# Causal latent attention of a prompt: the value product turned round and given to halves of the TensorE array, the weight sums carried with it, and three engines' turns rearranged

## The reference

```
q = (rmsnorm(cq) @ w_qb)              # 64 + 32 columns a head; the 32 are rotated
s = q_lat . ckv + q_pe . kpe          # masked where k_pos > q_pos, times MLA_SCALE
p = softmax(s)                        # over the keys
o_lat = p @ ckv ; o = o_lat @ w_uv    # 64 columns a head
```

## Time and profile before

| | us |
|---|---|
| median of 3 runs | 3236.84 (3233.66 to 3237.91) |
| the profiled execution | 3235.72 |
| its span | 3234.1 |

### The profile page before, as it was taken

One profiled execution on the slowest core, in us unless ns is written; L12 is line 12 of the kernel. 1 busy time (PEld: TensorE's weight loads), 2 busy tenths in 40 slices (PEclk: granted clock), 3 DMA queues, 4 the chain that ended last, 5 costly groups with the idle time before them and its releaser, 6 DMA issues. The chain is left out here.

```text
span 3234.1 us, 51727 instructions
## 1 busy us (share of the span) xinstructions
PE 3056.2 (95%) x21218; PEld 2736.5 (85%) x21218; DVE 1802.0 (56%) x3078; ACT 929.1 (29%) x1550; POOL 244.0 (8%) x280
## 2 busy tenths in 40 slices
PE   6987899998999999999989779989999999999998
PEld 5975577667999999999979546776699999999998
DVE  4856677553454545544566757865535545444554
ACT  4034444552311111111220444445423111111113
POOL 2000001540000000000020000025300000000000
PEclk8986999999999999999989779999999999999998
DMA  4112101762111111111031310047521111111201
GB/s 104 46 38 55 21 5 54 253 220 68 33 53 40 46 53 52 47 40 40 23 51 38 65 39 7 5 136 232 168 62 40 52 47 53 47 40 40 59 28 71
DMA packets 226587, 207.99 MB, mean 64 GB/s; under 512 B 50260, under 2 KB 195796, under 8 KB 226148
## 3 DMA queue, kind: packets, MB, share of 16 engines
q1 hardware_dynamic: 200744, 119.38, 13.6%
q0 software_dynamic: 25600, 85.11, 8.5%
HBM read 193.58 MB, written 11.05 MB: 63 GB/s over the span
## 5 line engine op out<-in xcount | busy, mean ns | idle before, releaser
L189 PE MATMUL ps<-streamH,upH 128*128 128x344 f32 x2112 | 449.2, 321 | 6.3 <-issue 5.0
L189 PE MATMUL ps<-streamH,upL 128*128 128x344 f32 x2112 | 447.4, 320 | 0.0
L189 PE MATMUL ps<-streamL,upH 128*128 128x344 f32 x2112 | 446.1, 320 | 0.0
L2266 ACT ACTIVATE upH<-hc 128x1024 fp32r<-128x1024 f32 x88 | 93.4, 1061 | 967.7 <-PE ps L189 967.7
L189 PEld LDWEIGHTS ps<-streamH,upH 128*128 128x128 f32 x2112 | 354.6, 188 | 8.7 <-issue 6.4
L189 PEld LDWEIGHTS ps<-streamH,upL 128*128 128x128 f32 x2112 | 356.1, 189 | 0.0
L189 PEld LDWEIGHTS ps<-streamL,upH 128*128 128x128 f32 x2112 | 352.8, 188 | 0.0
L2430 DVE TENSOR_TENSOR xT<-xT,ps 128x1032 f32<-128x1032 f32 x176 | 216.0, 1228 | 227.6 <-PE ps L189 227.6
L443 PE MATMUL ps<-inH,inW 128*128 128x344 f32 (+1 forms) x1248 | 234.1, 323 | 31.3 <-DVE inW L497 31.3
L2391 DVE TENSOR_TENSOR hc<-ps,rstd 128x1032 f32<-128x1032 f32 x44 | 54.2, 1232 | 370.7 <-PE ps L189 370.7
L443 PEld LDWEIGHTS ps<-inH,inW 128*128 128x128 f32 (+1 forms) x1248 | 198.9, 183 | 38.4 <-DVE inW L497 32.3
(11 more groups left out here) (472 smaller groups left out, 4899.4 us busy)
## 6 DMA issues: line engine op xcount, KB each, us to landing
hc<-in_w_ffn_in SPq DMA_DIRECT2D x88, 512.0 KB, 4.6
hc<-in_w_ffn_out SPq DMA_DIRECT2D x44, 512.0 KB, 3.7
big<-in_w_in SPq DMA_DIRECT2D x22, 512.0 KB, 3.9
stream_raw<-in_w_out SPq DMA_DIRECT2D x16, 512.0 KB, 4.0
big<-in_x_prompt SPq DMA_DIRECT2D x2, 2048.0 KB, 9.9
out_y_prompt<-big SPq DMA_DIRECT2D x8, 512.0 KB
scratch_y<-hc SPq DMA_DIRECT2D x16, 136.0 KB, 3.2
scratch_u<-wring SPq DMA_DIRECT2D x4, 516.0 KB, 3.1
```

What stands on the lines that cost most here:

```text
L189: last = pe.matmul(self.ps[:, bank + n, 0:NCOL], w, x[:, n * NCOL:(n + 1) * NCOL], start=(k == 0 and i == 0), stop=(k == len(terms) - 1 an ...
L2266: act.activation(upH[u][:, :, :], raw[u], ACT.Copy).then_inc(g_wh[u], 1)
```

## The change

- Four units make a **group**: `order` is now, for j = 0 to 3, for each head z, the blocks q = 7-j and q = j. Within a group the units A, B, C, D are (head 0, large), (head 0, small), (head 1, large), (head 1, small).
- `values(i)` works for a whole group. The 64 columns of `vt` are stationary (128 x 64), and p^T moves (128 columns). Head 0 writes partitions 0 to 63 of bank 7 and head 1 partitions 64 to 127, so each works on half of the array's columns, their products written in turn. The result has features on partitions. `outputs` and `otok` go away.
- The reciprocal of a row's sum must then lie along the columns: `reciprocals(u)` writes it 64 times over (128 x 64 from a broadcast source) to `rden`; `values(i)` first turns the two 128 x 128 tiles of `rden` into bank 7; ACT `factors(i)` copies them to `rT` (256 columns); DVE `output(i)` multiplies bank 7 by `rT` straight into `hc` (256 columns).
- p^T of a group is kept in four tiles, filled afresh only when the values of the group before are done. DVE `copies` takes the first bank of a large unit (512 columns), ACT `copies` all others.
- Scores run three units ahead: even units in banks 0 to 3, odd ones (at most 512 columns) in bank 4; p^T goes through banks 5 and 6; bank 7 is shared by the values and the steps, each of which waits until what was there before is drained.
- Ten steps instead of eleven: keys in two pieces of 512 columns instead of three of up to 344. They stand at units 0, 1, 2, 4, 5, 6, 8, 9, 10 and 12 of a pair.

```diff
-        otok = [take(D_MODEL).rearrange("p (q c) -> p q c", q=QT) for _ in range(2)]
+        small_pT = [take(512) for _ in range(2)]
+        rden = [take(P) for _ in range(2)]
+        rT = take(2 * P)
...
-        prob, pT = [T(16), T(17)], [T(18), T(19)]
...
-        order = [(v % 2, QT - 1 - v // 2 if v % 2 == 0 else v // 2) for v in range(NV)]
+        order = [(z, q) for j in range(4) for z in range(2) for q in (QT - 1 - j, j)]
...
-        STEPS = "DAAADDDAAAD"
+        copied_by = ["DA"[g] if u % 2 == 0 else "A" for u in range(NU) for g in range(banks_of[u])]
+        STEPS = "DAAADDDAAD"
         NS = len(STEPS)
-        step_at = {v: v - 2 for v in range(2, 1 + NS)}
-        step_at[NS + 2] = NS - 1
+        step_at = {v: j for j, v in enumerate((0, 1, 2, 4, 5, 6, 8, 9, 10, 12))}
+        VALUES_BANK = 7
...
+        step_of, values_of = {(0, j): j for j in range(NS)}, []
+        for u in range(NU):
+            p, v = u // NV, u % NV
+            if v in step_at and p + 1 < PAIRS:
+                step_of[p + 1, step_at[v]] = len(kinds)
+                kinds += STEPS[step_at[v]]
+            if v % 4 == 3:
+                values_of.append(len(kinds))
+                kinds += "V"
...
+        def copied(eng, at):
+            eng.wait_ge({"A": e_ta, "D": e_te}[copied_by[at]], copied_by[:at + 1].count(copied_by[at]))
+
+        def score_banks(u):
+            return ps[:, 2 * (u // 2 % 2):2 * (u // 2 % 2) + 2, :].rearrange("p b n -> p (b n)") if u % 2 == 0 else ps[:, 4, :]
+
+        def slot(kind, u):
+            return st[:, 4 * kind + u % 4:4 * kind + u % 4 + 1]
         chunk = lambda c: slice(c * NCOL, (c + 1) * NCOL)
-        kchunk = lambda c: slice(c * NCOL, min((c + 1) * NCOL, SEQ))
+        kchunk = lambda c: slice(c * 512, (c + 1) * 512)
...
-                    elif j in (7, 8, 9):
+                    elif j in (7, 8):
...
-                def outputs(p, half):
-                    k = out_of[p, half]
-                    drained(pe, k - 1)
-                    pe.wait_ge(e_oe, NV * p + (12, 16)[half])
-                    for i, q in enumerate(((2, 3, 4, 5), (0, 1, 6, 7))[half]):
-                        last = pe.transpose(ps[:, 7, i * P:(i + 1) * P], otok[p % 2][:, q, :], ident)
-                    last.then_inc(e_ax, 1)
...
-                    if u >= 2:
+                    if u % 2 == 0 and u >= 4:
+                        pe.wait_ge(e_p, u - 3)
+                    if u % 2 == 1 and u >= 2:
                         pe.wait_ge(e_p, u - 1)
...
-                        last = pe.matmul(ps[:, 2 * (u % 2) + c // 512, 0:w], query[p % 2][z][0:KQ, q * P:(q + 1) * P],
+                        last = pe.matmul(score_banks(u)[:, c:c + w], query[p % 2][z][0:KQ, q * P:(q + 1) * P],
...
-                            pe.wait_ge(e_te, at - 1)
+                            copied(pe, at - 2)
...
-                def values(u):
-                    p, z, q = units[u]
-                    pe.wait_ge(e_te, first_bank[u + 1])
-                    if u >= 1:
-                        pe.wait_ge(e_oe, u)
-                    h = 2 * p + z
-                    for kb in range(q + 1):
-                        last = pe.matmul(ps[:, 6, 0:V_DIM], pT[u % 2][:, kb * P:(kb + 1) * P], vt[:, kb, h * V_DIM:(h + 1) * V_DIM],
-                                         start=(kb == 0), stop=(kb == q))
+                def values(i):
+                    p, j = i // 4, i % 4
+                    drained(pe, values_of[i] - 1)
+                    pe.wait_ge(e_r, 4 * i + 4)
+                    for w in range(2):
+                        pe.transpose(ps[:, VALUES_BANK, (2 * w + 1) * P:(2 * w + 2) * P], rden[w], ident)
+                    for at in (first_bank[4 * i + 4] - 1, first_bank[4 * i + 2], first_bank[4 * i + 3] - 1):
+                        copied(pe, at)
+                    for w, q in ((1, QT - 1 - j), (0, j)):
+                        for kb in range(q + 1):
+                            for z in range(2):
+                                h = 2 * p + z
+                                last = pe.matmul(ps[64 * z:64 * z + 64, VALUES_BANK, 2 * w * P:(2 * w + 1) * P], vt[:, kb, h * V_DIM:(h + 1) * V_DIM],
+                                                 pT[w][z][:, kb * P:(kb + 1) * P], start=(kb == 0), stop=(kb == q))
                     last.then_inc(e_o, 1)
...
-                scores(0)
-                scores(1)
+                for u in range(3):
+                    scores(u)
...
                 for u in range(NU):
                     p, v = u // NV, u % NV
                     transposes(u)
-                    if u + 2 < NU:
-                        scores(u + 2)
-                    if u >= 1:
-                        values(u - 1)
-                    if v == 1 and p:
-                        outputs(p - 1, 1)
+                    if u + 3 < NU:
+                        scores(u + 3)
                     if v in step_at and p + 1 < PAIRS:
                         step(p + 1, step_at[v])
-                    if v == 14:
-                        outputs(p, 0)
-                values(NU - 1)
-                outputs(PAIRS - 1, 1)
+                    if v % 4 == 3:
+                        values(u // 4)
...
-
-                def outputs(p, half):
...
+                    if u >= 4:
+                        act.wait_ge(e_r, u - 3)
...
-                def output(u):
+                    act.activation(prob[u % 2][:, 0:n], score_banks(u)[:, 0:n], ACT.Exp, bias=slot(0, u), scale=MLA_SCALE,
+                                   accum_out=slot(1, u)).then_inc(e_p, 1)
+
+                def copies(u):
                     p, z, q = units[u]
-                    act.wait_ge(e_r, u + 1)
-                    act.wait_ge(e_o, u + 1)
-                    act.activation(otok[p % 2][:, q, z * V_DIM:(z + 1) * V_DIM], ps[:, 6, 0:V_DIM], ACT.Copy,
-                                   scale=st[:, 4 + u % 2:5 + u % 2]).then_inc(e_oe, 1)
-                for j in (1, 2, 3, 7, 8, 9):
+                    if u // 4:
+                        act.wait_ge(e_o, u // 4)
+                    for g in range(banks_of[u]):
+                        at = first_bank[u] + g
+                        w = (min(4 * g + 4, q + 1) - 4 * g) * P
+                        if copied_by[at] == "A":
+                            act.wait_ge(e_t, at + 1)
+                            act.activation(pT[1 - u % 2][z][:, 4 * g * P:4 * g * P + w], ps[:, 5 + at % 2, 0:w], ACT.Copy).then_inc(e_ta, 1)
+
+                def factors(i):
+                    act.wait_ge(e_o, i + 1)
+                    if i:
+                        act.wait_ge(e_oe, i)
+                    act.activation(rT.rearrange("p (w c) -> p w c", w=2),
+                                   ps[:, VALUES_BANK, :].rearrange("p (w x c) -> p w x c", w=2, x=2)[:, :, 1, :], ACT.Copy).then_inc(e_rt, 1)
+                for j in (1, 2, 3, 7, 8):
...
                 for u in range(NU):
                     p, v = u // NV, u % NV
-                    if u >= 1:
-                        output(u - 1)
+                    if u and u % 4 == 0:
+                        factors(u // 4 - 1)
+                    copies(u)
                     if u + 2 < NU:
                         exponentials(u + 2)
-                    if v == 1 and p:
-                        outputs(p - 1, 1)
                     if v in step_at and p + 1 < PAIRS and STEPS[step_at[v]] == "A":
                         drain(p + 1, step_at[v])
-                    if v == 14:
-                        outputs(p, 0)
-                output(NU - 1)
-                outputs(PAIRS - 1, 1)
+                factors(NU // 4 - 1)
...
-                    two = ps[:, 2 * (u % 2):2 * (u % 2) + 2, :].rearrange("p b n -> p (b n)")
+                    two = score_banks(u)
...
+                    s.link(dve.reduce_max(slot(2, u), two[:, 0:n], AX))
...
                 def reciprocals(u):
+                    p, z, q = units[u]
                     dve.wait_ge(e_p, u + 1)
-                    if u >= 2:
-                        dve.wait_ge(e_oe, u - 1)
-                    dve.reciprocal(st[:, 4 + u % 2:5 + u % 2], st[:, 2 + u % 2:3 + u % 2]).then_inc(e_r, 1)
+                    if u // 4:
+                        dve.wait_ge(e_o, u // 4)
+                    dve.reciprocal(rden[1 - u % 2][:, 64 * z:64 * z + 64], slot(1, u).to_broadcast([P, 64])).then_inc(e_r, 1)

                 def copies(u):
-                    p, z, q = units[u]
-                    for g in range(banks_of[u]):
-                        at = first_bank[u] + g
-                        w = (min(4 * g + 4, q + 1) - 4 * g) * P
-                        dve.wait_ge(e_t, at + 1)
-                        if u >= 2:
-                            dve.wait_ge(e_o, u - 1)
-                        dve.tensor_copy(pT[u % 2][:, 4 * g * P:4 * g * P + w], ps[:, 4 + at % 2, 0:w]).then_inc(e_te, 1)
-                for j in (0, 4, 5, 6, 10):
+                    at = first_bank[u]
```

(26 more changed lines are left out.)

56 lines of the change are left out of this document (18 added, 38 removed).

## The result

Over 18 executions each, the changed kernel takes 3231.19 us at the median (3225.82 to 3234.74) where the kernel before takes 3236.79: a ratio of 0.9981, 95% interval 0.9972 to 0.9990. Two more rounds on other chips gave 0.9990 (0.9980 to 0.9999) and 0.9988 (0.9979 to 0.9998). So some 3 to 6 us are gained where 15.8 were forecast. The profiled execution took 3230.60 us.

The account below looks back on a forecast made before the run. PE bounds the kernel now; afterwards a DVE-PE ring sets the loop: 166.4 + 21 + 5 - 3 = 189.4 us against 197.6. With +0.3 before the loop, a layer gains 7.9, both 15.8: 3221 us, range 3184 to 3256.

Parts of the forecast that it names:

- What bounds the kernel: In the mla_prompt loop before the change: PE is the bound, with work in flight 192.1 of 197.6 us.
- PE's sum: PE's work in a layer's loop: 165.6 us instead of 197.6, with the values' two column tiles overlapping.
- Rival 4: Values on PE: the tiles don't overlap, a group is 1.96 us longer, 31 a layer: 3284 us; 4%.
- The wide reciprocal: DVE's reciprocal of 64 columns: taken as 0.55 us, bounds 0.22 and 0.62, 35.2 us a layer.
- ACT: ACT in the loop: gets 48 bank copies, stays near 90 of 190 us, hides behind DVE except for factors.
- The ring: DVE and PE wait for each other in each group: 7.3 plus 3.1, 10.4 us a group; loop 189.4 us.
- The clock: PE's granted clock in the loop: expected to stay at 0.99 or 1.00, below 0.95 being rival 3.
- rival 3: Granted clock falls inside the loop, about 3 us each; slower from three a layer; four to eight give 3245 to 3269; 15%.
- my case: The whole kernel: each layer gains 7.9 us, both 15.8, median 3221; 50%, within 3203 to 3236.
- The unchanged stages: Stages outside mla_prompt: nothing else changes, so no gain or loss was counted for them.
- Rival 1: PE stays the bound: a wide reciprocal of 0.22 us shrinks the ring by 21 a layer, to 168: 3181 us; 13%.
- Rival 2: Ring has more waits than counted: half a microsecond more a group, 16 in all: 3237 us, no change; 18%.

Follow-up runs that it names:

- best: Changed kernel with one-column reciprocals spread by TensorE, D's reciprocal issued ahead of the next unit's maxima, and C's first bank copied by ScalarE: 3182.05 us, 0.9836.
- heads: Changed kernel with the two inner loops of the values swapped, all key blocks of one head before the other's: 3264.90 us, 1.0093.
- filler: Changed kernel with two throwaway products of 512 columns in PE's wait ahead of the values of groups j = 2, pairs 0 to 2: 3223.32 us, 0.9968.
- narrow: Changed kernel with one reciprocal a row, spread over 64 columns and turned by four small TensorE products a group: 3205.97 us, 0.9909.
- cheap: Changed kernel with a copy of the same shape in place of each wide reciprocal, so the output is not divided: 3208.28 us, 0.9922.
- early: Changed kernel with D's reciprocal issued ahead of the maxima of the unit behind it on DVE's queue: 3216.88 us, 0.9945.
- act_copies: Changed kernel with the first bank of unit C copied by ScalarE instead of VectorE: 3208.85 us, 0.9924.
- early_copies: Changed kernel with D's reciprocal issued ahead of the next unit's maxima and C's first bank copied by ScalarE: 3194.04 us, 0.9877.

## Why the prediction was wrong, point by point

- **What bounds the kernel:** right. PE was the bound, and is not after.
- **PE's sum:** right in kind. The loop has 168.1 us busy (165.6 summed; 165.8 at full clock in best). The overlap was right, 2.12 us a group. So was the reference for "no overlap", 0.109 a record: within one half heads shows 0.11. Rival 4 itself, with no overlap at all, was not run; heads keeps a part of it and comes to 3265.
- **The wide reciprocal:** 546 ns against 550. The slope between the reciprocals of 4 and 16 columns held to 64. The Trainium skill's page "VectorE: DVE Perf Modes", section "Walkthrough: the 8-slice pipeline in each mode", gives a reciprocal a repeat count of 8; the 0.68 us that I had estimated from it as 8 cycles a column is not what the row shows.
- **ACT:** its count was wrong. It copies 64 banks a layer and not 48 (two rows of 32 in the trace), and is busy for 95.4 us instead of some 90. It did not decide anything: the copies that PE waited for were DVE's.
- **The ring:** right. Groups of the last pair last 10.15, 10.05 and 9.96 us against 10.4, DVE is busy for 148.5 against 150.4. The path through the copy of C's bank and the transposes of D was not in the turn that I added up. The loop is 191.8 against 189.4; less its two falls of the clock, 188.9.
- **The clock: the step that failed.** My sum had it at 0.99 as before and kept the falls for rival 3, at 3 us each and as slower than before from three a layer. There are two a layer, at 1.45 us each, and filler takes three of the four away. So the likeliest course was between my case and the rival: 2.9 us a layer, 5.8 in all, that belonged in the sum. The prologue, 0.5 instead of 0.3, adds 0.4. That takes 15.8 to 9.6, and the traces show 10.
- **The unchanged stages: the second step.** I took them to cost what they cost before. They cost 4 to 7 us more, and the traces show 5 of them in the two sample stages, which stand longer at half clock. By the measure of the loop (5.8 us lost in 13.6 at half clock), the 6 to 8 us more of half clock outside it come to 3. Why the clock falls there for longer is open: the position explains one pair of runs and not the others. So is why narrow and best lose nothing there but gain 7 and 3.
- **Rival 1** (a reciprocal of 0.22 and PE as the bound, 3181): its price was wrong, and cheap shows that its end was, too. With 0.19 us in the place of each reciprocal the kernel comes to 3208, since the second path takes over. It took narrow, early and act_copies together to come to 3182.
- **Rival 2** (half a microsecond more of waits in a group): no; the groups of the last pair are 0.3 shorter than counted. That its time, 3237, lies nearer to the measured one than mine is chance.

## What to carry over

When an edit takes the bound off an engine, follow what its new order ties together and add up one turn of that ring: here that gave the period of a group to 4%, and showed where to look next: the order on one queue and the choice of the copying engine (early_copies) were worth some 35 us more, where the change gave 3 to 6. Add up the second path as well: here it took over as soon as the reciprocals were cheap. Price the waits on TensorE that a ring creates not at their length alone, but with what the granted clock does behind them: here waits of 1.8 us stood ahead of falls that cost 1.45 us each. And don't read a gain of a few us off two profiles: measure the changed part in the trace and the whole over many executions, and expect them to differ: half of what narrow gained lies outside the part that it changed.

## What the hardware showed

- A reciprocal on DVE costs 6.1 to 6.2 ns a column from 4 to 64 columns (178 to 546 ns), a copy of 64 columns in SBUF 186 ns in all.
- Value records of 64 weight columns and 128 moving ones follow each other every 0.11 us on one half of the array and every 0.056 us when they alternate between the halves (32 in 1.79 us). Changing the order of two loops cost 1.36 us in a group of 36.
- A stationary operand that repeats one column 64 times is loaded like any other, in narrow (137 ns at the median, as the value tiles), and spreads a value over 64 partitions: the eight records of a group take 519.12 - 518.64 = 0.48 us.
- Two products with no use in a wait of up to 1.8 us, in three groups of each layer, made the kernel 7 to 9 us faster, 4.6 of them in the changed part by the granted clock behind them.
- The sample stage, whose instructions no edit touches, takes 198.7 to 201.6 us in two traces of before and 202.2 to 202.8 in three of after, with 14 to 20 and 19 to 23 us of it at half clock.
